# Queries, keys and values of the second block: another order of blocks, later transposes, and PSUM copies on ScalarE

## What is computed

```python
def rms_norm(x, gain):
    xf = x.astype(jnp.float32)
    y = xf * lax.rsqrt(jnp.mean(xf * xf, axis=-1, keepdims=True) + NORM_EPS)
    return (y * gain.astype(jnp.float32)).astype(x.dtype)
...
        proj = h @ w_in[layer]
        (q_m, k_m, v_m, q_f, k_f, v_f, f_logit, q_c, a_m, a_f, a_c) = jnp.split(proj, split_points, axis=-1)

        q_m = partial_rope(rms_norm(split_heads_2(q_m, MOBA_HEADS), g_q_moba[layer]))
        k_m = partial_rope(rms_norm(split_heads_2(k_m, MOBA_HEADS), g_k_moba[layer]))
        y_m = moba_attention(q_m, k_m, split_heads_2(v_m, MOBA_HEADS))

        log_f = jax.nn.log_sigmoid(f_logit.astype(jnp.float32)
                                   + b_forget[layer].astype(jnp.float32)).transpose(0, 2, 1)
        q_f = rms_norm(split_heads_2(q_f, FOX_HEADS), g_q_fox[layer])
        k_f = rms_norm(split_heads_2(k_f, FOX_HEADS), g_k_fox[layer])
        y_f = fox_attention(q_f, k_f, split_heads_2(v_f, FOX_HEADS), log_f)
...
        mk = rms_norm(split_heads_2(mk, MEM_HEADS), g_k_mem[layer])
        q_c = rms_norm(split_heads_2(q_c, MEM_HEADS), g_q_mem[layer])
        y_c = memory_attention(q_c, mk, split_heads_2(mv, MEM_HEADS))
```

## Time and profile before

| | us |
|---|---|
| median of the three runs | 1549.68 |
| lowest and highest | 1547.8, 1551.15 |
| the profiled execution | 1552.51 |
| its span in the trace | 1550.7 |
| the stage in that trace: product 0 starts | 1077.47 |
| the first scores start | 1183.57 |

### The profile page before, as it was taken

The page is one execution under the profiler, slowest core; times in us unless marked ns, Lnnn a source line. Parts: engine busy times, 40 slices in busy tenths (PEclk is TensorE's granted clock), DMA queues, the critical chain, the costliest instruction groups (busy, mean ns, idle before and its releaser), DMA issues. The chain is left out here.

```text
span 1550.7 us, 20944 instructions
## 1 busy us (share of the span) xinstructions
PE 1470.4 (95%) x8247; PEld 1268.2 (82%) x8247; DVE 1154.2 (74%) x1266; ACT 751.7 (48%) x785; POOL 4.1 (0%) x7
## 2 busy tenths in 40 slices
PE   3998999999999997999999999989899999999999
PEld 3876799899898877887888788877677778799997
DVE  5888677776778764988888989887896776555544
ACT  1534333334472633777677677655343443343332
POOL 0000000000000000000000000000000000000000
PEclk9999999999999997999999999999999999999999
DMA  8776379877654561998998999954244335445652
GB/s 310 256 292 223 127 242 298 282 255 245 217 192 160 190 217 36 331 332 302 351 338 302 339 338 315 339 211 136 82 163 159 113 110 165 160 138 175 198 170 106
DMA packets 198424, 345.73 MB, mean 223 GB/s; under 512 B 11632, under 2 KB 90064, under 8 KB 193232
## 3 DMA queue, kind: packets, MB, share of 16 engines
q1 hardware_dynamic: 190592, 339.76, 64.4%
q10 hardware_dynamic: 7760, 4.97, 1.1%
HBM read 343.65 MB, written 1.05 MB: 222 GB/s over the span
## 5 line engine op out<-in xcount | busy, mean ns | idle before, releaser
L1951 DVE TENSOR_TENSOR wlo<-raw,whi 128x2048 fp32r<-128x2048 f32 (+2 forms) x220 | 479.9, 2193 | 160.3 <-ACT whi L630 156.2
L630 ACT ACTIVATE whi<-raw 128x2048 fp32r<-128x2048 f32 (+2 forms) x220 | 402.9, 1836 | 356.9 <-PE ps L1211 229.2
L1209 PE MATMUL ps<-whi,AH 128*128 128x512 f32 (+1 forms) x816 | 323.0, 396 | 12.3 <-DVE wlo L1951 9.3
L1210 PE MATMUL ps<-wlo,AH 128*128 128x512 f32 (+1 forms) x816 | 313.2, 384 | 0.0
L1211 PE MATMUL ps<-whi,AL 128*128 128x512 f32 (+1 forms) x816 | 313.1, 384 | 0.0
L1209 PE MATMUL ps<-AH,whi 128*128 128x256 f32 x896 | 256.0, 286 | 2.1 <-DVEq L2051 1.5
L1210 PE MATMUL ps<-AL,whi 128*128 128x256 f32 x896 | 254.6, 284 | 0.0
L1211 PE MATMUL ps<-AH,wlo 128*128 128x256 f32 x896 | 254.6, 284 | 0.0
L1209 PEld LDWEIGHTS ps<-whi,AH 128*128 128x128 f32 x816 | 154.7, 190 | 53.5 <-DVE wlo L1951 17.0
L1211 PEld LDWEIGHTS ps<-whi,AL 128*128 128x128 f32 x816 | 154.4, 189 | 28.6
L1209 PEld LDWEIGHTS ps<-AH,whi 128*128 128x128 f32 x896 | 172.6, 193 | 3.7 <-DVEq L2051 1.8
(11 more groups left out here) (324 smaller groups left out, 1531.1 us busy)
## 6 DMA issues: line engine op xcount, KB each, us to landing
raw<-in_ada_w SPq DMA_DIRECT2D x48, 1024.0 KB, 5.4
raw<-in_w_in SPq DMA_DIRECT2D x26, 1024.0 KB, 5.2
raw<-in_moe_w_up SPq DMA_DIRECT2D x24, 1024.0 KB, 7.2
raw<-in_h_w_in SPq DMA_DIRECT2D x16, 1024.0 KB, 5.7
raw<-in_moe_w_gate SPq DMA_DIRECT2D x16, 1024.0 KB, 7.5
raw<-in_moe_w_down SPq DMA_DIRECT2D x16, 1024.0 KB, 6.4
acc<-in_moe_w_down SPq DMA_DIRECT2D x16, 1024.0 KB, 8.2
raw<-in_m_w_in SPq DMA_DIRECT2D x12, 1024.0 KB, 5.7
```

The lines of the kernel that those rows point to most:

```text
L630: act.activation(whi[:, h, 0:n], raw_at[s][:, 0:n], ACT.Copy).then_inc(w_hi, 1)
L1209: pe.matmul(o, sh, mh, start=first, stop=False)
L1210: pe.matmul(o, sh, ml, start=False, stop=False)
L1951: dve.tensor_tensor(wlo[:, h, 0:n], raw_at[s][:, 0:n], whi[:, h, 0:n].bitcast(fp), ALU.subtract)\
```

## The change

It has five parts.
1. The blocks are made in the order 0, 1, 3, 4, 6, 2, 5 (`QKV_ORDER`), so both value blocks come last. `NORMED` has the `mkv` keys at its end. Products 0 to 5 each have a norm behind them: blocks 0, 1, 3, 4, 6, and the `mkv` keys behind product 5.
2. The transposes of the block normed behind product j-2 stand inside product j, between its two units. The last ones follow product 6, and the filler behind them is 3 matmuls where there were 14 ahead of them.
3. ScalarE copies products (`block_out`) and transposed blocks (`transposed_out`) out of PSUM. VectorE copies none.
4. `forget_gates` is cut in two: `forget_first` behind norm 0, `forget_sums` behind norm 2. Its last eight instructions, which write `fox_l`, are on ScalarE behind root 3 (`fox_rows`). Only the scores of the second branch wait for `fox_set`.
5. `hi` and `lo` of the stage are written one unit earlier: unit 2 before the loop, then units 2j+3 and 2j+4 in the pass of product j.

```diff
+QKV_ORDER = (0, 1, 3, 4, 6, 2, 5)
+NORMED = ((0, 0, A_D, 0, 0), (1, A_D, A_D, 0, 1), (3, 2 * A_D, A_D, 1, 0), (4, 3 * A_D, A_D, 1, 1),
+          (6, 4 * A_D, C_D, 2, 0), (None, 4 * A_D + C_D, C_D, 2, 1))
...
+            first_unit = w.unit - LEAD
+            hi(w)
+
+            def block_out(j):
+
+                act.wait_ge(w_used, first_unit + 2 * j + 2)
+                bank = 2 * ((PAIR_QKV + (0, 2, 3, 5, 7, 9, 11)[j]) % 4)
+                link(act.activation(qkv[:, QKV_ORDER[j]], ps[:, bank:bank + 2, :], ACT.Copy))
+                act.sem_inc(ps_free, 1)
+
+            def transposed_out(n):
+
+                b, which = NORMED[n][3:5]
+                act.wait_ge(tp_done, QK_TPS + n)
+                bank = 2 * ((PAIR_QKV + (4, 6, 8, 10, 12, 13)[n]) % 4)
+                act.activation(acc[:, b, 1024 * which:1024 * which + 1024].rearrange("p (b n) -> p b n", b=2),
+                               ps[:, bank:bank + 2, :], ACT.Copy).then_inc(qk_set, 1)
+                act.wait_ge(qk_set, n + 1)
+                act.sem_inc(ps_free, 1)
...
+            def fox_rows():
+
+                act.wait_ge(fcum_set, 1)
+                for h in range(A_HEADS):
+                    ins = act.activation(fox_l[:, h, :], fcum, ACT.Identity, bias=cst[:, C_FOX + 10 + h:C_FOX + 11 + h],
+                                         scale=cst[:, C_FOX + 2 + h:C_FOX + 3 + h])
+                ins.then_inc(fox_set, 1)
+
             for j in range(7):
-                his(w, 2)
-                if j == 0:
+                hi(w)
+                if j == 1:
...
+                if j < 6:
+                    hi(w)
+                block_out(j)
+                if j >= 2:
+                    transposed_out(j - 2)
+                if j < N_NORMED:
+                    block_squares(j)
+                if j == 3:
+                    fox_rows()
+            transposed_out(N_NORMED - 1)
...
             for j in range(7):
-                m_matrix(w, 1)
+                bank = pair(w)
+                m_unit(w, bank, 0, 4, KT)
+                if j >= 2:
+                    qk_transposes(j - 2)
+                m_unit(w, bank, 4, 4, KT)
...
-                if j - 1 in NORM_BEHIND:
-                    qk_transposes(NORM_BEHIND[j - 1])
-            keep_busy(w, 14)
-            qk_transposes(len(NORMED) - 1)
+            qk_transposes(N_NORMED - 1)
+            keep_busy(w, 3)
             pe.wait_ge(qk_set, 6)
-            pe.wait_ge(fox_set, 1)
...
-            first_unit = w.unit - LEAD
+            lo(w)
             for j in range(7):
-                los(w, 2)
-                dve.wait_ge(w_used, first_unit + 2 * j + 2)
-                bank = bank_of(w)
-                free(w, dve.tensor_copy(qkv[:, j], ps[:, bank:bank + 2, :]))
-                if j in NORM_BEHIND:
-                    dve.sem_inc(qk_raw, 1)
+                lo(w)
+                if j < 6:
+                    lo(w)
+                w.next_pair()
+                if j >= 2:
+                    w.next_pair()
+                if j < N_NORMED:
+                    norm_block(j)
                 if j == 0:
-                    forget_gates()
-                if j - 1 in NORM_BEHIND:
-                    copy_block(NORM_BEHIND[j - 1])
-                if j in NORM_BEHIND:
-                    norm_block(NORM_BEHIND[j])
-            copy_block(len(NORMED) - 1)
+                    forget_first()
+                if j == 2:
+                    forget_sums()
+            w.next_pair()
```

More of the change, by code:

```diff
@@ L52 @@
             (2 * A_HEADS, C_HEADS, C_D, False, False))
-NORMED = ((0, 0, A_D, 0, 0, 0), (1, A_D, A_D, 0, 1, 1), (None, 4 * A_D + C_D, C_D, 2, 1, 2),
-          (3, 2 * A_D, A_D, 1, 0, 3), (4, 3 * A_D, A_D, 1, 1, 4), (6, 4 * A_D, C_D, 2, 0, 6))
-NORM_BEHIND = {entry[5]: n for n, entry in enumerate(NORMED)}
+QKV_ORDER = (0, 1, 3, 4, 6, 2, 5)
+NORMED = ((0, 0, A_D, 0, 0), (1, A_D, A_D, 0, 1), (3, 2 * A_D, A_D, 1, 0), (4, 3 * A_D, A_D, 1, 1),
+          (6, 4 * A_D, C_D, 2, 0), (None, 4 * A_D + C_D, C_D, 2, 1))
+N_NORMED = len(NORMED)
 PAIR_HEADS = 2 + 2 + 1 + 2 + 2 + 1 + 2 + 1
@@ L75 @@
 E_PAIRS_2 = 24
-PAIR_ATT = PAIR_MOE + E_PAIRS * N_EXPERTS + 2 + 2 + 2 + 7 + 1 + 6
+PAIR_QKV = PAIR_MOE + E_PAIRS * N_EXPERTS + 2 + 2 + 2
+PAIR_ATT = PAIR_QKV + 7 + 1 + 6
 PAIR_FFN2 = PAIR_ATT + 12 + 2 + 2 + 2
@@ L112 @@
 FEATURE_TPS = (2, 4, 6, 8, 10, 12, 14, 22, 24)
+QK_TPS = FEATURE_TPS[-2] - 7
 FEATURE_PAIRS = (3, PAIR_HEADS + 1, PAIR_FFN - 1, PAIR_LEVELS - 1,
@@ L316, in build @@
         e_hh, t_split, t_back = sem("e_hh"), sem("t_split"), sem("t_back")
-        qk_raw, qk_ready, qk_set = sem("qk_raw"), sem("qk_ready"), sem("qk_set")
+        fcum_set, qk_ready, qk_set = sem("fcum_set"), sem("qk_ready"), sem("qk_set")
         fox_set = sem("fox_set")
@@ L565, in _ @@
                 m_unit(w, w_mkv, k0, 4, 512)
-            m_matrix(w, w_in2, 0, 6)
-            m_matrix(w, w_in2, Q_MEM, 1)
+            for blk in QKV_ORDER:
+                m_matrix(w, w_in2, Q_MEM if blk == 6 else 512 * blk, 1)
             for kind, b, c, k0 in ATT_UNITS:
@@ L1137, in _, with block_squares @@
             second_half(vec[:, V_GMIX:V_GMIX + 8])
+            first_unit = w.unit - LEAD
[13 more added lines that the diff above has]
+                act.sem_inc(ps_free, 1)
+            def block_squares(n):
+                at_least(act, qk_ready, n)
+                src = mkv[:, 0] if NORMED[n][0] is None else qkv[:, NORMED[n][0]]
+                act.activation(tok(GB[:, 0, :]), src, ACT.Square).then_inc(sq_done, 1)
+                root(2 * (512 // NORMED[n][2]))
+            def fox_rows():
[4 more added lines that the diff above has]
+                ins.then_inc(fox_set, 1)
             for j in range(7):
-                his(w, 2)
-                if j == 0:
+                hi(w)
+                if j == 1:
                     act.wait_ge(g_vec, 4)
@@ L1800, in scores @@
                 at_least(pe, t_exp, 2 * n)
+                if fox:
+                    pe.wait_ge(fox_set, 1)
                 for i, (c0, width) in enumerate(((0, n0), (n0, 256))):
@@ L2869, in _, with forget_first @@
             to_features(w, vec[:, V_GMIX:V_GMIX + 8])
-            def forget_gates():
+            def forget_first():
                 dve.wait_ge(late_small, 11 * 16)
@@ L2876, in forget_gates, with forget_sums @@
                 both(dve.scalar_tensor_tensor(frow[:, 1, :], frow[:, 0, :], -1.0, frow[:, 0, :], ALU.mult, ALU.max), g_vec, 4)
+            def forget_sums():
                 dve.wait_ge(g_act, 4)
@@ L2888, in forget_gates @@
                 dve.tensor_scalar(fox_r, fcum, cst[:, C_FOX:C_FOX + 1], cst[:, C_FOX + 1:C_FOX + 2],
[L2889 to L2893, removed]
+                                  ALU.mult, ALU.add).then_inc(fcum_set, 1)
             def norm_block(n):
```

16 lines of the change are left out of this document (1 added, 15 removed).

## The result

The changed kernel takes 1529.76 us (median of 4 runs, 1527.27 to 1531.54); the kernel before took 1550.41 in the 4 runs beside it (1547.8 to 1555.21). The ratio is 0.9866, with a 95% interval of 0.9844 to 0.9889. It is 20.65 us faster. The forecast was 1530.4 us, 19.3 less than before.

The account below looks back on a forecast made before the run. The prediction took VectorE, slower than TensorE by 0.4 us a pass, to make TensorE wait. A stage 16.6 us shorter plus 2.7 us by the clock, 19.3 in all, took 1549.7 to 1530.4 us, range 1527 to 1537.

Parts of the forecast that it names:

- Bound: In the old stage VectorE's pass takes 12.4 us against TensorE's 12.0, so VectorE is the slower by 0.4 us.
- PE up to product 6: TensorE runs five products and five sets of transposes without waits; product 6 ends at 1163.2, 9.9 us earlier.
- the transposes inside a product: On TensorE each set of eight transposes adds 1.03 us to a product of 10.99 us.
- The copies: ScalarE's copies out of PSUM take 1.02 to 1.2 us each; its pass is 7.6 us of 12.0.
- The deadlines: Work for TensorE is ready in time: norm 5 with 1.0 us to spare, unit 9 1.9, unit 11 2.2.
- The end: Behind product 6 three ScalarE copies hold the first scores until 1167.0, so the stage ends 16.6 us earlier.
- The clock: A single TensorE gap of 1.4 us ahead of the first scores keeps the full clock, saving 2.7 us more.
- Rival 1: The clock falls all the same at the first scores after the 1.4 us gap: 1533.1 us; chance 0.12.
- Sum: Over the whole kernel, 16.6 and 2.7 us make 19.3 us saved, none lost behind the stage: 1530.4 us.
- Rival 4: ScalarE becomes the bound: felt past 12.0 us a pass, forecast lost at 15.2, slower above that; chance 0.03.

## Why the prediction was right

**Bound.** VectorE was what TensorE waited for. With the copies back on it 17.3 of 20.5 us are gone, and moving only its forget gate in the old kernel turned a wait of 5.05 us into one of 5.3 at another place. Load is not all of it, though: with the copies off VectorE and the old order kept, norm 0 was still 5.03 us late. With the new order and the copies on it, that wait was gone, but weight units came 3.5 and 2.9 us late instead. Up to slot 1, the copies alone bring 5.55 us, the rest of the change alone 3.21, both together 20.51.

**PE up to product 6.** I had 1163.2 - 1077.5 = 85.7 us from product 0; it was 84.6. The term that was mis-sized is the transposes inside a product: 1.03 us each by their row, but the next matmul starts 0.79 after they do (1106.37 to 1107.16), and five of them make the 1.2 us. The time between two starts would have been the right thing to read. Every set of this stage before had a wait behind it, but the six transposes at 1200.14 in the earlier trace rows did not: the next matmul starts at 1200.72, which makes 0.77 us for eight.

**The copies.** 1005 and 1026 ns by line on ScalarE, where the earlier trace rows had 1023:

```profile
L1152 ACT ACTIVATE Z<-ps 128x1024 f32<-128x1024 f32 x7 | 7.0, 1005 | 2.6 <-PE ps L1256 2.6
...
L1160 ACT ACTIVATE acc<-ps 128x1024 f32<-128x1024 f32 x6 | 6.2, 1026 | 0.7
L1176 ACT ACTIVATE t_high<-TS,cst 128x256 fp32r<-128x256 f32 x8 | 4.0, 589 | 0.0
```

`fox_rows` took 4.0 us where I had 3.4.

**The deadlines** all held. Norm 5 was done 0.9 us ahead of its transposes (1.0 forecast); unit 9 was 1.5 us early (1.9); unit 11 only 1.1 (2.2). The longer `fox_rows` is not the reason: the `lo` of unit 11 was done 66.15 us after the start of product 0, 66.1 in the forecast. Its deadline had come 1.1 us nearer, mostly by the four sets of transposes ahead of it that cost 0.79 us and not 1.03. So the mis-sized term helped the time and took room from the deadlines. Doubling the copies broke exactly the one with the least room.

**The end.** 3.70 us from product 6 to the scores, 3.8 forecast. The timeline of ScalarE:

```profile
1160.07 1.02 ACT L1152 ACTIVATE Z<-ps 128x1024 f32<-128x1024 f32 x1 [2.60 <-PE ps L1256]
1161.22 2.16 ACT L1160 ACTIVATE acc<-ps 128x1024 f32<-128x1024 f32 x2
1163.56 1.91 ACT L637 ACTIVATE whi<-raw 128x2048 fp32r<-128x2048 f32 x1 [0.18 <-ACT acc L1160]
1165.49 1.28 ACT L1206 ACT_TABLE_LOAD   x1
1166.78 0.37 ACT L1206 ACTIVATE Z<-ps,col 128x128 f32<-128x128 f32 x1
```

Three copies in a row, then the scores. The gap was 1.37 us where 1.4 was forecast.

**The clock.** It stayed at 2.4 GHz, and slot 1 came 12.46 us after slot 0 and not 15.17: 2.71 us, 2.7 forecast. Rival 1 was out here, and it hung on the filler: without it the gap was 1.3 us longer, and the slow clock was back. That the clock would be kept was read off one gap at the start of product 0; the traces agree, but they give no rule that it follows from.

**Sum.** From product 0: 17.80 us to the scores (16.6 forecast, the difference being the transposes), 2.71 by the clock, 20.51 in all against 19.3. The run time came nearer (1529.76 against 1530.4) than that, and this is partly luck: the fourth run of before raised its median from 1549.68 to 1550.41, and the start of product 0, ahead of the change, moves by up to 6.8 us between traces.

**A rival that was sized wrongly.** Rival 4 said that ScalarE would be felt only past 12.0 us of work a pass, and that the gain would be lost at 15.2. With 9.9 us busy in a plain pass (11.0 with the gaps), 13.4 of the 20.5 were gone. Two things failed in it. It compared plain passes only, and left out `fox_rows` and the exponential, logarithm and table loads, with which two passes had 13.6 and 13.8 us of work. And it compared loads: a plain pass took 12.0 us for 9.9 of work, since copy, squares, norm and `lo` follow one another over two engines, and what has to be short enough is that chain against its deadline. How much of the 13.4 us each of the two is worth was not measured apart. The deadlines were in the prediction, further up; the rival did not use them. Its side of the forecast was not touched by this, since real copies took 1.0 us.

**Open.** Why the clock was kept over gaps of 1.51 and 1.25 us in one kernel and lost over 1.69 and 1.48 in another, or kept over a single one of 3.52 and lost over 2.91 and 2.67, was not settled. The old kernel was profiled once. Its 2.7 us at the first scores need not come in every execution: the same two gaps cost 1.5 us in the run with the forget gate behind norm 0. The fifth part of the change (`hi` and `lo` one unit earlier) was not tested by itself. The split of the gain into parts is from single traces each; the constant 351.9 us behind slot 1 is what makes them comparable.

## What to carry to other kernels

When one engine is late in many places, moving its work about can just move the wait (5.05 us at one place, 5.3 at another), and taking work off it can leave the worst wait standing (5.03 us). Here it took lighter work and a better order together. Test a part both ways, alone in the old kernel and undone in the new: the copies were worth 5.6 us one way and 17.3 the other, and two parts that cost 0.2 and 1.9 us alone cost 7.4 together. For an engine that takes work over, check each chain against its deadline, and every pass and not only the plain one: with 9.9 us of work in a plain pass against TensorE's 11.8, and near 14 in two others, 13 us were lost.

## What the runs showed of the hardware

- Ahead of the first scores, a single gap of 1.37 us in TensorE's work kept the clock at 2.4 GHz, and behind one of 2.67 us the scores and part of the product behind them ran at 1.2 GHz, 3.1 us of time. Fillers worth 1.3 us of work were the difference.
- The length of a gap did not decide by itself: with the copies on VectorE, the clock stayed at 2.4 GHz behind a gap of 3.52 us and fell behind one of 2.91 us. The same pair of gaps, 1.69 and 1.48 us, brought 1.2 GHz from the first scores on in the trace before and 0.7 us later in the old kernel with the forget gate behind norm 0.
- After a gap of 8.70 us, eight transposes took 1.97 us and three fillers 2.77, and the two groups of scores behind them took 0.58 and 0.70, so the clock was back. Here the fillers ahead of the work that counts bore the slow stretch.
- Eight transposes of 128 x 128 in front of a matmul of 512 columns cost 0.79 us from start to start, though their row says 1.03.
- Where the eight operand rows of `fox_l` are written, 128 x 256 each, ScalarE took 4.0 us for them and VectorE 2.7.
